# Linear layers as single f32 matmuls of unsplit operands, with one ring of weight blocks for all stages

## The reference

```python
# first layer
xn = rms_norm(h, mix_pre_g);  proj = xn @ w_in             # z 1024, xbc 1536, dt 16, q, k, v 1024 each
y_ssd = ssd_mixer(z, xbc, dt, ...)                         # conv, chunks of 128, state, gate, norm
y_sb  = rms_norm(stick_breaking_attention(q, k, v))        # 16 heads of 64, blocks of 128 queries
h = h + rms_norm(concat([y_ssd, y_sb]) @ w_out)            # 2048 -> 1024
gu = rms_norm(h) @ w_up                                    # 1024 -> 2 x 2816
f = (gelu(causal_dwconv(gu[:D_FF])) * gu[D_FF:]) @ w_down  # 2816 -> 1024
h = h + rms_norm(f)
# second layer
u = rms_norm(h) @ w_in_2                                   # queries, keys, values, gates; 16- and 64-wide ranks
gla_out, rwkv_out = gla_chunked(...), rwkv7_scan(...)      # chunks of 64
out = rms_norm(h + concat([gla_out, rwkv_out]) @ w_out_2)
```

## Time and profile before

| | before |
|---|---|
| median of 3 runs | 2577.19 us (2571.52 to 2577.98) |
| the profiled execution | 2572.99 us |
| its span, first to last instruction | 2571.2 us |
| mean granted clock of TensorE | 0.979 |
| busy: PE, DVE, ACT, POOL | 2444.2, 1355.7, 976.8, 941.2 us |
| moved by DMA | 182.25 MB |

### The profile page before, as it was taken

One profiled execution on the slowest core, in us unless ns is written; L12 is line 12 of the kernel. 1 busy time (PEld: TensorE's weight loads), 2 busy tenths in 40 slices (PEclk: granted clock), 3 DMA queues, 4 the chain that ended last, 5 costly groups with the idle time before them and its releaser, 6 DMA issues. The chain is left out here.

```text
span 2571.2 us, 45422 instructions
## 1 busy us (share of the span) xinstructions
PE 2444.2 (95%) x18736; PEld 1569.1 (61%) x18736; DVE 1355.7 (53%) x1441; ACT 976.8 (38%) x1712; POOL 941.2 (37%) x711
## 2 busy tenths in 40 slices
PE   7999988999999988998999999999999999999997
PEld 5667755666666645665666666544854444568856
DVE  7666763434444346377444444324778847335544
ACT  3226754555555555353111111223554422213321
POOL 4443236556665564004444444200025533101150
PEclk9999999999999989999999999999999999989999
DMA  3122110000000001441111111232633541133411
GB/s 126 41 83 74 58 50 25 26 18 26 26 21 22 17 1 61 134 150 58 49 49 49 49 49 53 88 98 75 207 108 99 164 132 50 58 86 88 147 55 66
DMA packets 110774, 182.25 MB, mean 71 GB/s; under 512 B 26480, under 2 KB 76800, under 8 KB 109200
## 3 DMA queue, kind: packets, MB, share of 16 engines
q1 hardware_dynamic: 110608, 179.89, 21.8%
HBM read 154.10 MB, written 25.76 MB: 70 GB/s over the span
## 5 line engine op out<-in xcount | busy, mean ns | idle before, releaser
L1357 DVE TENSOR_TENSOR_SCAN att_kept<-att_keep 128x143 f32<-128x143 f32 (+7 forms) x128 | 171.1, 1342 | 315.6 <-ACT att_keep L1274 315.5
L218 PE MATMUL ps<-x_lo,whi_z 128*128 128x342 f16 x1008 | 310.5, 308 | 0.0
L217 PE MATMUL ps<-x_hi,whi_z 128*128 128x342 f16 x1008 | 310.0, 307 | 0.2 <-POOL wlo_z L191 0.2
L219 PE MATMUL ps<-x_hi,wlo_z 128*128 128x342 f16 x1008 | 309.5, 307 | 0.0
L1121 POOL TENSOR_TENSOR att_beta<-att_beta,att_kept 128x256 f32<-128x256 f32 (+7 forms) x128 | 195.5, 1527 | 223.5 <-DVE att_kept L1357 202.5
L1154 PE MATMUL ps<-x_hi,whi_z 128*128 128x348 f16 x576 | 181.5, 315 | 14.0 <-POOL wlo_z L1111 9.4
L2360 PE MATMUL ps<-second_x_hi,whi_z 128*128 128x512 f16 (+1 forms) x496 | 184.9, 373 | 2.4 <-DVE second_x_lo L1530 1.4
L2362 PE MATMUL ps<-second_x_hi,wlo_z 128*128 128x512 f16 (+1 forms) x496 | 184.6, 372 | 0.0
L2361 PE MATMUL ps<-second_x_lo,whi_z 128*128 128x512 f16 (+1 forms) x496 | 184.6, 372 | 0.0
L1156 PE MATMUL ps<-x_hi,wlo_z 128*128 128x348 f16 x576 | 181.0, 314 | 0.0
L1155 PE MATMUL ps<-x_lo,whi_z 128*128 128x348 f16 x576 | 180.9, 314 | 0.0
(11 more groups left out here) (542 smaller groups left out, 6004.1 us busy)
## 6 DMA issues: line engine op xcount, KB each, us to landing
wraw_z<-in_w_up SPq DMA_DIRECT2D x44, 512.0 KB, 3.7
wraw_z<-in_w_second SPq DMA_DIRECT2D x30, 512.0 KB, 3.8
wraw_z<-in_w_qkv SPq DMA_DIRECT2D x24, 512.0 KB, 3.7
wraw_z<-in_w_down SPq DMA_DIRECT2D x20, 512.0 KB, 3.6
raw_down<-in_w_down SPq DMA_DIRECT2D x20, 512.0 KB, 4.0
seg<-dt_a_sums SPq DMA_DIRECT2D x18, 512.0 KB, 4.3
wraw_z<-in_w_out SPq DMA_DIRECT2D x18, 512.0 KB, 3.7
wraw_out<-in_w_out SPq DMA_DIRECT2D x18, 512.0 KB, 3.6
```

What stands on the lines that cost most here:

```text
L217: nc.tensor.matmul(out, hi, xhi, start=(k == 0), stop=False)
L218: nc.tensor.matmul(out, hi, xlo, start=False, stop=False)
L219: return nc.tensor.matmul(out, lo, xhi, start=False, stop=(k == L.parts * L.kb - 1))
L1357: nc.vector.tensor_tensor_scan(out[:, 1:t.keys], x, x, 1.0, ALU.mult, ALU.min).then_inc(s_scan, 1)
```

## The change

- Every linear product is one f32 matmul of the unsplit weight block and the unsplit activations. All cuts of weights and activations, their buffers and WSCALE are gone; norms write x directly (`normalize`, `link_pre`).
- One tensor of four weight slots serves all stages in turn. A block is fetched when the products of the block that held its slot are done, not when that block is cut. The down-projection uses a ring of 8 slots, the second layer's input one of 4; the last projection's blocks have places of their own.
- The out-projection fetches each of its 13 half blocks once and holds them. Three more, the first (SSD) halves of its blocks 5, 6 and 7, are multiplied in attention's last steps (EARLY = 3: nine more groups of `linear`, 72 products of 348 columns), and DVE adds those sums in `out_phase`.
- SSD stage: the last chunk makes no new state; filler comes after `turn_x`; ACT makes `end(c+1)` earlier; DVE's order changes.
- Up-projection: DVE writes f from PSUM in four pieces in place of one piece, two f16 copies by ACT and two subtractions.
- Second input: the block of which 16 rows are used is multiplied in four groups of 32 columns of the array, and the gate's matrix is repeated over the partitions to sum them.

The core of the diff:

```diff
@@ products: start and up-projection
-                hi, lo = (x[:, w, j * P:(j + 1) * P] for x in (L.hi, L.lo))
-                xhi, xlo = (x[:, t0 + n * tb:t0 + (n + 1) * tb] for x in xs(k))
-                nc.tensor.matmul(out, hi, xhi, start=(k == 0), stop=False)
-                nc.tensor.matmul(out, hi, xlo, start=False, stop=False)
-                return nc.tensor.matmul(out, lo, xhi, start=False, stop=(k == L.parts * L.kb - 1))
+            return nc.tensor.matmul(banks(s)[:, n, 0:tb], L.raw[:, s, k * P:(k + 1) * P], x[:, k, t0 + n * tb:t0 + (n + 1) * tb],
+                                    start=(k == 0), stop=(k == DB - 1))
@@ stream_weights, SP
-            sp.wait_ge(L.cut, i * SLOTS + (s + 1))
+            sp.wait_ge(L.products, i * SLOTS + (s + 1 + SLOTS))
@@ attention_phase, POOL
-                for part in range(3):
-                    cut(2, part)
-                cut_by_pool(nc, pool, N)
...
+                for n in range(STEPS):
+                    for a in range(2):
+                        weights(n, a)
@@ attention_phase, PE
-                        if g < QKV_B * NT:
+                        if g < (QKV_B + EARLY) * NT:
                             linear(g, DB * i // len(rounds), DB * (i + 1) // len(rounds))
@@ out_phase, SP
-                for y in OUT_LOADS[SLOTS:]:
-                    i = y.load
-                    if i >= RING:
-                        sp.wait_ge(s_cut, i - RING + 1)
-                    sp.dma_start(part_of("raw", i), L.w[2 * y.b + y.half]).then_inc(s_landed[i % RING], 16)
...
+                for i in range(SLOTS, len(OUT_LOADS)):
+                    b, half = OUT_LOADS[i]
+                    sp.dma_start(slots[i], Lo.w[2 * b + half]).then_inc(s_landed[i], 16)
@@ ffn_up_phase, DVE
-                    nc.vector.scalar_tensor_tensor(fm(f[:, :]), psum_tn(S, 1)[:, :, 0:FT], 1.0 / WSCALE, fm(acc[:, :]),
-                                                   ALU.mult, ALU.mult).then_inc(s_f, 1)
...
+                    for k, (n, c0, c1) in enumerate(pieces):
+                        r, w = k // 2, c1 - c0
+                        last = nc.vector.tensor_tensor(row(S.f, base, i, r)[:, at[r]:at[r] + w], psum_tn(S, 1)[:, n, c0:c1],
+                                                       acc[:, n * FT + c0:n * FT + c1], ALU.mult)
@@ second_in_phase, PE
+                def narrow(i):
...
+                    for n in range(2):
+                        for j0 in range(0, DB, groups):
+                            for a in range(groups):
+                                j = j0 + a
+                                last = nc.tensor.matmul(banks(i)[a * GROUP:(a + 1) * GROUP, n, :], L.raw[:, i % L.n, j * P:j * P + GROUP],
+                                                        S.x[:, j, n * BANK:(n + 1) * BANK], start=(j0 == 0), stop=(j0 > 0), skip_group_check=True)
```

More of the change, by code:

```diff
@@ L121, in blk, with linear_buffers @@
     return t[:, bass.ds(b, 1), :].rearrange("p a n -> p (a n)")
-def linear_buffers(nc, ctx, w, first, kb, tag, side="left", parts=1, raw=None, like=None):
+def linear_buffers(nc, ctx, w, tag, raw=None, side="left"):
     L = Names()
[L133 to L142, removed]
+    L.w, L.fetched = w, False
+    L.raw = raw if raw is not None else ctx.enter_context(nc.sbuf_tensor(f"wraw_{tag}", [P, SLOTS, DB * P], F32, side=side))
+    L.n = L.raw.shape[1]
+    L.landed = [ctx.semaphore(f"w_landed{s}_{tag}") for s in range(L.n)]
     L.products = ctx.semaphore(f"products_{tag}")
@@ L170, in cut_first @@
[L170 to L179, removed]
@@ new lines, in one, with product @@
+        pe.wait_ge(L.landed[s], i * 16 + 16)
+        def product(n, k):
+            return nc.tensor.matmul(banks(s)[:, n, 0:tb], L.raw[:, s, k * P:(k + 1) * P], x[:, k, t0 + n * tb:t0 + (n + 1) * tb],
+                                    start=(k == 0), stop=(k == DB - 1))
+        if await_input:
+            for k in range(DB):
+                ready(pe, k)
+                for n in range(nt):
+                    last = product(n, k)
+        else:
+            for n in range(nt):
+                for k in range(DB):
+                    last = product(n, k)
@@ L234, in products @@
+        last.then_inc(L.products, 1)
     start = first // SLOTS
@@ L1445, in out_parts @@
         x.use = i
-        same = [y for y in loads[-2:] if (y.b, y.half) == (x.b, x.half)]
-        x.load = same[0].load if same else len(loads)
-        x.fresh = not same
-        if not same:
-            loads.append(x)
-    last_use = {x.load: x.use for x in parts}
-    return units, parts, loads, last_use
-OUT_UNITS, OUT_PARTS, OUT_LOADS, OUT_LAST = out_parts()
-OUT_PASS = DB - OUT_FULL
+        if (x.b, x.half) not in loads:
+            loads.append((x.b, x.half))
+        x.load = loads.index((x.b, x.half))
+    return units, parts, loads
+OUT_UNITS, OUT_PARTS, OUT_LOADS = out_parts()
+EARLY_UNITS = [u for u, (b, _) in enumerate(OUT_UNITS) if b >= DB - EARLY]
 def of_unit(u):
@@ L1926, in down_loads @@
     for u, (b, _) in enumerate(DOWN_UNITS):
-        again = u > 0 and DOWN_UNITS[u - 1][0] == b
+        held = {x: i for i, x in enumerate(loads) if i >= len(loads) - RING}
+        again = all((b, q) in held for q in range(len(DOWN_PARTS)))
         for q in range(len(DOWN_PARTS)):
             if again:
-                of_part[u, q] = of_part[u - 1, q]
+                of_part[u, q] = held[b, q]
             else:
@@ L2168 @@
 HALF = SUB // 2
+GROUP = 32
 R0, GLA0 = 1, 1 + 3 * RWKV_P
@@ L3464, in program @@
             s_parked_h = second.semaphore("h_parked")
-            rows, L, down = ffn(nc, S, A, second, layer, Lz, Lu, hs, ssq, parked_h, s_parked_h)
+            rows, L, down = ffn(nc, S, A, second, layer, Lu, hs, ssq, parked_h, s_parked_h)
             second_layer(nc, S, A, second, L, rows, down, parked_h, s_parked_h, out)
```

1010 lines of the change are left out of this document (332 added, 678 removed).

## The result

The changed kernel takes 2988.16 us (median of 4 runs, 2986.65 to 2990.52) against 2574.36 us for the kernel before in the same comparison: 1.161 times, 95% interval 1.159 to 1.163. It is slower by 414 us; the prediction has 454. The profiled execution took 2988.07 us, its span 2986.3 us, at a mean granted clock of 0.995.

A forecast was written before the change was run, and what follows sets the result against it. The prediction took PE, busy for 95% of the span, to bound the kernel: 539 us of added PE work less 85 us won back gave +454 us, a forecast of 3028 us, range 2965 to 3100.

The forecast's parts named there:

- The price: All linear stages: one f32 product costs 0.585 us at 348 columns against 0.444 for three f16 matmuls, 0.141 more.
- The rival by which an f32 product is a single pass: Whole kernel: an f32 product is one pass of records, not two, in long runs; perhaps 2050 us; chance 1%.
- the two signs of being wrong: Up-projection's stage not 570 to 600 us long (the price), or PE's idle time over 100 us (the waits).
- The sum of what is won back: All stages: removed waits and clock loss of PE give back 85 us of at most 178.
- What stays is chains of ACT and DVE that have no cut in them ... the copies of turned attention weights: Several stages: PE's waits on such chains, also sums of squares between stages and the ends, remain; nothing won back there.
- The waits for x_decayed ... stood behind cuts on POOL's queue: SSD stage: six waits, 8.1 us, go with the cuts; with longer fillers the stage wins back 14 us.
- The out-projection, 10 of 20: Out-projection: 10 us won back of 15.4 idle and 5 of clock loss, 4.5 + 4.5 on cuts.
- Attention's front: Start of attention: PE's 9.4 us wait for POOL's wlo_z and clock loss go with the cuts; 14 us won back.
- Attention's tail: Attention's last steps, 900 to 980 us: the 72 moved products serve as filler; 22 of 24 us come back.
- The switch gaps of 0.09 us: Steps from f16 to f32 on PE: left out of the sum; all gone would be some 18 us.
- That nothing is won back: Whole kernel: new waits replace the old, or DVE's scan paces attention's tail; 3113 us; chance 8%.
- More is won back: Whole kernel: f32 products keep PE full, clock stays at 1.00, switch gaps vanish; 2950 to 2990 us; chance 15%.

The follow-up runs named there:

- t3: Changed kernel with the 72 early out-projection products run in one piece behind attention's last step, not spread over the last pair's steps; 3013.75 us.
- t1: Changed kernel with three bfloat16 matmuls (one on upper halves, two with zeros as moving operand) for each f32 linear product, no cuts; 2490.38 us, one run.
- t5: Changed kernel with dummy POOL operations, awaited by nobody, at the old places of the cuts in the SSD stage and attention; 2987.23 us.
- t6: Changed kernel with the SSD stage's orders as before, one bank for the last outputs, still without cuts or last chunk's state; 2998.43 us.
- t8: Kernel before, all cuts kept, with POOL's new order at attention's front and the SSD stage's new orders, without the last chunk's state; 2546.0 us, ratio 0.9903.
- t10: Changed kernel with 20 more 512 KB transfers of out-projection weights, memory to memory, in that stage; 2987.23 us.
- t4: Kernel before with POOL cutting attention's weight block 3 after the third subtraction of the activations, not the last; 2562.16 us, ratio 0.9967.
- t9: Kernel before with t8's changes and the narrow block as three f16 matmuls per group in four column groups; 2542.87 us, ratio 0.9877.
- t2: Changed kernel with one bfloat16 matmul on the upper halves of weights and x for each f32 linear product; 1664.85 us, one run.

## Why the prediction was right, and where it was off

**The price was right, and it is nearly the whole answer.** 0.585 us for 348 columns, read from the first two blocks of the kernel before (24 products, 48 records), gave 0.575 for 342; the changed kernel shows 0.575. The term of the up-projection was 1008 x 0.14 = 141 for the loop, and it grew by 138.4, with 2.5 us less idle time. The Trainium skill's "FP8 and Floating Point Precision", section TensorE Precision Notes, says that true FP32 makes four passes through the array. Four times the 0.145 us of an f16 matmul of 342 columns here would be 0.580 us (0.435 / 3 from the earlier trace rows; an estimate from that page), and the trace agrees. The rival by which an f32 product is a single pass was wrong for the reason given: it counts records, and a product has two. (Its 3860 products of 348 columns are 3909 by the prediction's own counts; the forecast does not use the number.) Neither of the two signs of being wrong came: up's loop is 582 us long, and PE's idle time 46.5.

**The sum of what is won back was 31 us too small** (85 against 116), and that is most of the 39 by which the sum missed; the other 8 are PE's own work, 539 against 531, and were not traced. By stage the won-back time is 13 too small in attention, 9 in the out-projection, 6 in SSD. Three steps of it:

- *"What stays is chains of ACT and DVE that have no cut in them ... the copies of turned attention weights"*: it is true that no cut is in them, and false that they stay. Of the 9.7 us for att_w_meta 6.6 are in the tail: t3 has them again to the digit without cuts, so the moved products took them away. The 3.1 us ahead of the tail are 4.0 in t1 with short fillers and 0.7 now, so there it is the length of the filler. Of the missing cuts nothing is seen in it.
- *"The waits for x_decayed ... stood behind cuts on POOL's queue"*: wrong in mechanism. t5 loads POOL's queue again and nothing comes back; t6 restores only orders and the waits return; t8 frees the stage with all cuts in place. The prediction gave 14 us to this stage; 20 came, some 10 of them by orders that the list of the change names and the sum leaves out. That its 14 was near is partly luck. The prediction read the releaser (POOL) and the queue's contents but not what POOL itself had been waiting for. Its other reason, the longer filler, is worth about 3 us (6.1 idle in t1 against 3.1).
- *The out-projection, 10 of 20*: a mis-sized term. 19 came: the 9 us of waits on cuts that it counted, and with them all of the clock loss and the waits for sums of squares (4.4 us in the kernel before), which it had left. t10 speaks against the saved traffic, and t1, with 3.7 us idle, against the length of the filler for all but 2 us. The new order of blocks and the missing cuts are not told apart.

Attention's front held in direction: the wait is gone, by t4 worth 8 us on the kernel before, without any change of the cutting. Attention's tail held in size: 22 to 24 expected, 25.6 measured by t3. The narrow block held (4.5 against some 3.6). "Nothing" held for the saved fetches; for the ring of four it was off by 4 us. The switch gaps of 0.09 us were rightly left out of the sum: in the changed kernel six f32 records of a filler, from 646.14 us, and the step to the next product of attention (L1019, at 647.99) take 1.85 us, where six steps of 0.2925 would be 1.76.

Of the 116 us single runs account for some 60: the filler in the tail for 22 (t3), the SSD stage's orders for 10 (t6), POOL's queue at attention's front for 8 (t4), the length of the fillers for 22 (t1). The rest is not told apart. The waits on cuts in the start, the out-projection, up and down are in it, since the instructions that they ended on are gone, but no run brings them back.

**The rivals.** That nothing is won back is excluded by the waits after. "More is won back" had the direction of the miss: 2988 lies at the upper edge of its 2950 to 2990, with the clock at 1.00 and 116 of 178 us back. Of its reasons the one about longer f32 products is 22 us by t1, the lesser part of the 116, and the one about switch gaps did not come true.

## What to carry to other kernels

On a kernel that PE bounds at 95%, price the new matmul from a matmul of the same type that already runs there, by distance of starts and per product of the program, not per record: that gave 539 us (531 came), and all else here is a correction of it. Waits are second. For each, look one step further back than the releaser: a queue full of other work is no proof that the work on it is what makes an instruction late; the idle time of the releaser ahead of that instruction tells. And try an order's change on the old kernel by itself: t9 takes 31 us off it without the change of the products.

## What was not expected of the hardware

- Reading every second 2-byte element for both operands cost a matmul little: t2's start 0.153 us apart where an f16 one on packed operands took 0.145, 6% more for 342 columns. In t1, where two of three have packed zeros as the moving operand, three took 0.440 against 0.435.
- Matmuls on four groups of 32 columns ran at once: in t9 48 f16 ones of 512 columns in 2.7 us, a group of four every 0.217 us, where one at full width takes 0.216. The 32 f32 records took 3.57 us, 0.45 for four, where one at full width takes 0.43.
- With f32 products throughout, the granted clock was 1.00 in every stage but down (0.99) and the last stretch, from 2675 us on (0.97), where it had been 0.97 or 0.98 in SSD, attention and out-projection. The kind of product alone does not decide it: t1 with short ones has 0.99, 1.00 and 1.00 there, and t3 with f32 ones falls to 0.83 where PE has gaps.
